# Per-tile order in a group norm's end, and a second PSUM bank with a split last step in a state space model's end

## The reference, cut to what matters

```python
mean = jnp.mean(y, axis=-1, keepdims=True)               # over a head of 64 channels
var = jnp.mean(jnp.square(y - mean), axis=-1, keepdims=True)
yn = ((y - mean) * lax.rsqrt(var + RW_GN_EPS)).reshape(B, T, D)
yn = yn * ln_w.astype(f32) + ln_b.astype(f32)
bonus = jnp.sum(rh * kh * r_k.astype(f32), axis=-1, keepdims=True) * vh
out = (yn + bonus.reshape(B, T, D)).astype(x.dtype) * g
return out @ w_o, v_first
```

```python
y = (einsum("blgp,ghp->blgh", s_re, c_re) - einsum("blgp,ghp->blgh", s_im, c_im) + d * uf)
y = jax.nn.gelu(y)
cu = jax.nn.silu(layer_norm(cu, conv_ln_g, conv_ln_b))
```

## Time and profile before

| | |
|---|---|
| median of 3 runs | 3901.69 us (3901.31 to 3909.06) |
| profiled execution | 3902.99 us, its span 3901.2 us |
| TensorE busy | 3577.1 us (92%) |
| VectorE busy | 2570.5 us (66%) |
| ScalarE busy | 1536.5 us (39%) |
| GpSimd busy | 1152.7 us (30%) |
| mean granted TensorE clock | 0.965 |
| group norm's end | from 2027.9 us to the first product of `at[2]` at 2110.91 us |
| the model's end | from 3567.1 us (`outputs(2)`) to the barrier behind 3602.4 us |

### The profile page before, as it was taken

One profiled execution on the slowest core, in us unless ns is written; L12 is line 12 of the kernel. 1 busy time (PEld: TensorE's weight loads), 2 busy tenths in 40 slices (PEclk: granted clock), 3 DMA queues, 4 the chain that ended last, 5 costly groups with the idle time before them and its releaser, 6 DMA issues. The chain is left out here.

```text
span 3901.2 us, 57647 instructions
## 1 busy us (share of the span) xinstructions
PE 3577.1 (92%) x24956; PEld 2905.9 (74%) x24956; DVE 2570.5 (66%) x2287; ACT 1536.5 (39%) x1634; POOL 1152.7 (30%) x521
## 2 busy tenths in 40 slices
PE   8999999999989998877777999999998999997997
PEld 6778788878767776666655788878886888875775
DVE  5554767687756857766655666678758888816532
ACT  5563432344534338744444433343443222113312
POOL 1125454555421211233322445445520000000211
PEclk9999999999999999999998999999999999997998
DMA  2112233344212245712113123253312222231322
GB/s 97 49 38 62 70 108 104 104 158 171 68 55 82 107 144 163 237 63 73 69 46 113 46 98 111 92 185 131 115 48 106 75 75 78 82 141 30 144 95 103
DMA packets 187037, 383.74 MB, mean 98 GB/s; under 512 B 16080, under 2 KB 84816, under 8 KB 181008
## 3 DMA queue, kind: packets, MB, share of 16 engines
q1 hardware_dynamic: 149216, 307.68, 23.8%
q10 hardware_dynamic: 37568, 72.36, 5.0%
HBM read 273.57 MB, written 105.91 MB: 97 GB/s over the span
## 5 line engine op out<-in xcount | busy, mean ns | idle before, releaser
L3817 POOL MEMSET ssm_toep<- 128x4096 f32 x1 | 3.5, 3512 | 545.7 <-POOLq L3516 545.7
L3403 DVE SCALAR_TENSOR_TENSOR H<-hy_cu,par,H 128x1024 f32<-128x1024 f32 x120 | 153.5, 1279 | 0.0
L269 POOL TENSOR_TENSOR wlo1C<-fast_raw,whi1C 128x1024 fp32r<-128x1024 f32 (+1 forms) x40 | 110.9, 2773 | 113.4 <-ACT whi1C L259 113.4
L269 POOL TENSOR_TENSOR wlo0B<-fast_raw,whi0B 128x1024 fp32r<-128x1024 f32 (+1 forms) x40 | 112.1, 2802 | 107.5 <-ACT whi0B L259 107.5
L3403 DVE SCALAR_TENSOR_TENSOR hy_odd<-hy_cu,par,hy_odd 128x1024 f32<-128x1024 f32 x112 | 143.3, 1280 | 0.0
L269 POOL TENSOR_TENSOR wlo1A<-fast_raw,whi1A 128x1024 fp32r<-128x1024 f32 (+1 forms) x40 | 111.4, 2785 | 105.6 <-ACT whi1A L259 105.6
L269 POOL TENSOR_TENSOR wlo1B<-fast_raw,whi1B 128x1024 fp32r<-128x1024 f32 (+1 forms) x39 | 107.9, 2766 | 114.3 <-ACT whi1B L259 114.3
L1007 DVE TENSOR_TENSOR fast_xl<-fast_xr,fast_xh 128x2048 fp32r<-128x2048 f32 (+1 forms) x42 | 127.5, 3059 | 21.3 <-ACT fast_xh L848 21.3
L269 POOL TENSOR_TENSOR wlo0A<-fast_raw,whi0A 128x1024 fp32r<-128x1024 f32 (+1 forms) x40 | 110.1, 2753 | 105.0 <-ACT whi0A L259 105.0
L269 POOL TENSOR_TENSOR wlo0C<-fast_raw,whi0C 128x1024 fp32r<-128x1024 f32 (+1 forms) x39 | 108.0, 2770 | 104.2 <-ACT whi0C L259 104.2
L942 DVE TENSOR_TENSOR fast_g<-fast_g,flow_rms 128x1024 f32<-128x1024 f32 x44 | 127.0, 2886 | 1.5
(11 more groups left out here) (1458 smaller groups left out, 11925.8 us busy)
## 6 DMA issues: line engine op xcount, KB each, us to landing
fast_raw<-ffn_in_dram SPq DMA_DIRECT2D x88, 512.0 KB, 3.8
fast_xr<-ffn_x SPq DMA_DIRECT2D x28, 1024.0 KB, 6.1
sc_ops<-rw_arbkv SPq DMA_DIRECT2D x15, 1280.0 KB, 7.2
fast_raw<-ffn_out_dram SPq DMA_DIRECT2D x32, 512.0 KB, 3.8
wraw1A<-hybrid_in_dram SPq DMA_DIRECT2D x24, 512.0 KB, 3.4
wraw1B<-hybrid_in_dram SPq DMA_DIRECT2D x24, 512.0 KB, 3.3
ffn_x<-fast_g ACTq DMA_DIRECT2D x22, 512.0 KB, 3.3
ffn_x<-fast_e ACTq DMA_DIRECT2D x22, 512.0 KB, 2.8
```

Of the source, the lines that this page charges most:

```text
L269: eng.tensor_tensor(self.slot(wlo, n), self.raw[n], self.slot(whi, n).bitcast(fp32), ALU.subtract)\
L3403: op = dve.scalar_tensor_tensor(out=acc, in0=c[:, j:j + T], scalar=w, in1=acc, op0=ALU.mult, op1=ALU.add)
L3817: pl.memset(toep[:, :, :], 0.0).then_inc(*tick("st_zero"))
```

## The change

In the group norm's end the three engines go tile by tile. VectorE does `gated(0)`, centres tiles 6 and 7, then `gated(k)` and `low(k - 1)` in turn. ScalarE takes `high(k)` between the roots. TensorE does `spreads(2)` ahead of all products and `spreads(3)` behind the product of tile 1. The low parts stay on VectorE.

In the state space model's end the outputs of odd k go to psC instead of psD, and wait for the copy of k - 2 rather than k - 1. The last `outputs(3)` is cut into two halves with `back(2)` between them. `back(3)` goes to psB and waits for the Ln that read psB. VectorE copies `outputs(2)` ahead of the scaled tiles, and makes six scaled tiles ahead of the copy of `outputs(3)` and two behind it.

```diff
                     sums(3)
-                    for q in range(DT // 2):
-                        if q == 0:
-                            W.begin(pe, at[0])
-                            W.begin(pe, at[1])
-                        for k in (2 * q, 2 * q + 1):
-                            pe.wait_ge(*after("ro_lo", k + 1))
-                            W.product(pe, at[0], k, *self.xs[k])
-                            W.product(pe, at[1], k, *self.xs[k])
-                        if q < 2:
-                            spreads(q + 2)
+                    spreads(2)
+                    W.begin(pe, at[0])
+                    W.begin(pe, at[1])
+                    for k in range(DT):
+                        pe.wait_ge(*after("ro_lo", k + 1))
+                        W.product(pe, at[0], k, *self.xs[k])
+                        W.product(pe, at[1], k, *self.xs[k])
+                        if k == 1:
+                            spreads(3)
...
                     squares(2)
+                    high(0)
                     roots(1)
-                    for q in range(DT // 2):
-                        high(2 * q)
-                        high(2 * q + 1)
-                        if q == 0:
-                            squares(3)
-                        if q + 2 < DT // 2:
-                            roots(q + 2)
+                    high(1)
+                    squares(3)
+                    high(2)
+                    roots(2)
+                    high(3)
+                    roots(3)
+                    high(4)
+                    high(5)
                     W.hi(act, 2)
+                    high(6)
+                    high(7)
...
-                    for q in range(DT // 2):
-                        gated(2 * q)
-                        gated(2 * q + 1)
-                        low(2 * q)
-                        low(2 * q + 1)
-                        if q == 0:
-                            centre(DT - 2)
-                            centre(DT - 1)
+                    gated(0)
+                    centre(DT - 2)
+                    centre(DT - 1)
+                    for k in range(1, DT):
+                        gated(k)
+                        low(k - 1)
+                    low(DT - 1)
...
-                        def outputs(k):
+                        def outputs(k, groups=range(8)):
...
+                            elif k == 1:
+                                pe.wait_ge(*after("sb_b", SU))
                             else:
-                                pe.wait_ge(*after("sy_c", 2 * k))
+                                pe.wait_ge(*after("sy_c", 2 * k - 2))
...
-                                to = ps[3][:, g % 2, q * P:(q + 1) * P]
+                                to = ps[3 - k % 2][:, g % 2, q * P:(q + 1) * P]
...
-                            pe.wait_ge(*after("su_c", SU) if k == 0 else after("sy_t", k))
+                            if k == 0:
+                                pe.wait_ge(*after("su_c", SU))
+                            elif k < SU - 1:
+                                pe.wait_ge(*after("sy_t", k))
+                            else:
+                                pe.wait_ge(*after("ln_log", 1))
...
-                        for k in range(SU + 1):
-                            if k < SU:
-                                outputs(k)
-                            if k > 0:
-                                back(k - 1)
-                            if k == 0:
-                                variance(0)
-                                variance(1)
-                            if k == 1:
-                                for m in range(2, DT):
-                                    variance(m)
+                        outputs(0)
+                        variance(0)
+                        variance(1)
+                        outputs(1)
+                        back(0)
+                        for m in range(2, DT):
+                            variance(m)
+                        outputs(2)
+                        back(1)
+                        outputs(3, range(4))
+                        back(2)
+                        outputs(3, range(4, 8))
+                        back(3)
...
-                        for k in range(4):
-                            normed(k)
                         outputs(2)
-                        for k in range(4, DT):
+                        for k in range(6):
                             normed(k)
                         outputs(3)
+                        for k in range(6, DT):
+                            normed(k)
```

More of the change, by code:

```diff
@@ L3855, in outputs @@
                                 pe.wait_ge(*after("st_in", 16 * SC))
-                            else:
-                                pe.wait_ge(*after("sy_c", 2 * k))
-                            for g in range(8):
+                            elif k == 1:
+                                pe.wait_ge(*after("sb_b", SU))
+                            else:
+                                pe.wait_ge(*after("sy_c", 2 * k - 2))
+                            for g in groups:
                                 q, rows = g // 2, slice(64 * (g % 2), 64 * (g % 2) + 64)
-                                to = ps[3][:, g % 2, q * P:(q + 1) * P]
+                                to = ps[3 - k % 2][:, g % 2, q * P:(q + 1) * P]
                                 pe.matmul(to, ut[:, 8 * k + g, :], toep[:, 8 * k + g, :], start=True, stop=False)
@@ L3863, in outputs @@
                                     mm = pe.matmul(to, ee[rows, k, z, q, 0:SN], cq[rows, k, z, q, SSM_H:], start=False, stop=(z == 1))
-                            mm.then_inc(*tick("pe_yc"))
+                            if groups[-1] == 7:
+                                mm.then_inc(*tick("pe_yc"))
                         def back(k):
                             pe.wait_ge(*after("sy_c", 2 * k + 2))
-                            pe.wait_ge(*after("su_c", SU) if k == 0 else after("sy_t", k))
+                            if k == 0:
[4 more added lines that the diff above has]
+                                pe.wait_ge(*after("ln_log", 1))
                             for i in range(SC):
-                                mm = pe.transpose(ps[0][:, i // 4, (i % 4) * P:(i % 4 + 1) * P],
+                                mm = pe.transpose(ps[k // (SU - 1)][:, i // 4, (i % 4) * P:(i % 4 + 1) * P],
                                                   yc[:, k, i, :, :].rearrange("p g h -> p (g h)"), ident)
@@ L3949, in _ @@
                             act.wait_ge(*after("pe_yt", k + 1))
-                            act.activation(y[:, k, :].rearrange("p (c i) -> p i c", i=SC), flat[0].rearrange("p (i c) -> p i c", i=SC),
+                            act.activation(y[:, k, :].rearrange("p (c i) -> p i c", i=SC), flat[k // (SU - 1)].rearrange("p (i c) -> p i c", i=SC),
                                            ACT.Gelu_apprx_tanh).then_inc(*tick("sy_t"))
@@ L3997, in outputs @@
                                 dve.tensor_copy(yc[:, k, :, e:8:2, :].rearrange("p i q h -> p q i h"),
-                                                ps[3][:, e, :].rearrange("p (q i h) -> p q i h", q=4, i=SC)).then_inc(*tick("sy_c"))
+                                                ps[3 - k % 2][:, e, :].rearrange("p (q i h) -> p q i h", q=4, i=SC)).then_inc(*tick("sy_c"))
                         ch(dve.memset(ee[:, :, :, :, 0:1], 0.0))
```

## The result

The change makes the kernel faster: 3873.01 us, the median of 4 runs (3864.44 to 3876.89), against 3901.5 (4 runs, 3899.82 to 3909.06) beside it, a ratio of 0.9922 with an interval of 0.9905 to 0.9938. Forecast were 3875 and a range of 3869 to 3884. The profiled execution took 3864.44 us, 38.5 less than the one of before (3902.99); it is the fastest of the four.

What follows compares the result with a forecast made beforehand. VectorE's order of work was taken to bound the group norm's end, and TensorE's wait for a copy and the lower clock the model's end. Gains of 15.2 + 11.6 = 26.8 us gave 3875 us, range 3869 to 3884.

Steps and rivals of the forecast that it cites:

- VectorE binds the first place: Group norm's end: VectorE's 41.6 us of work, two 0.8 us waits and 2.3 us of blocking set its end; gain 15.2 us.
- The collision: Group norm's end: GpSimd's low part of strip 2 blocks a VectorE operation through the shared port pair, costing 2.3 us.
- Rival (c): Group norm's end: GpSimd and VectorE do not collide; whole gain 29.1 us, time 3872.6; chance 0.08.
- The waits of TensorE: Group norm's end: TensorE's waits for the low parts shrink from 26.1 to some 15 us, each 1 to 4 us.
- The windows show a clock near 1.00: Group norm's end: the new profile's windows would show TensorE's granted clock near 1.00.
- no gap of 7 us is left: Group norm's end: TensorE's gaps become 1 to 3 us instead of 7 to 10, an argument against a low clock.
- rival (b): Group norm's end: clock falls between single products and stays low, TensorE binds; gain 5.2 there, 16.8 in all, 3884.9; chance 0.08.
- The model's end: State space model's end: `outputs(3)` follows `back(1)` without a wait and the clock stays at 1.00; gain 11.6 us.
- (a): Model's end: the clock falls though the gap is gone; gain 6.2 there, 21.4 in all, 3880.3; chance 0.13.
- The gain kept: Behind the group norm's end: TensorE has no gap for 44.1 us, so the 15.2 us gained there stay in the total.
- (d): Behind the group norm's end: its gain is given back later, only the model's end counts; 3890.1; chance 0.05.
- (e): Six strips of `at[2:]`: clock stays low there too, each strip losing 9.5 us; slower, 3942 with all six; chance 0.02.

Runs made afterwards that it cites:

- the filled gap: Changed group norm, old model's end, plus 12 unread products in TensorE's gap behind `back(1)`: first product of `outputs(2)` to SP's next-stage issue 27.42 us, 35.58 before.
- the bank alone: Changed group norm; of the model's end only psC/psD alternation, old orders kept: first product of `outputs(2)` to SP's next-stage issue 24.26 us, 24.18 with the whole change.
- The crossed kernels: Whole change with strip 2 late, but pairs kept with early centring, or tile order with late centring: first gated operation to first psC product 49.30 and 59.40 us.
- the four small edits: Against before: tiles 6 and 7 centred early, spreads(2) and spreads(3) one place earlier, pairs kept; psC for odd outputs: 3870.86 us, ratio 0.9915.

## Why the prediction was right, and where it wasn't

**VectorE binds the first place: right.** 41.6 us of work and two waits of 0.8 us were forecast; the waits are 0.88 and 0.81, at the root and at the high part that I named. psC's first product is 50.00 us behind the start, forecast 50.3 (2095.7 - 2045.42). The time itself came within 2 us of the 3875 forecast, and that is partly luck: the four executions lie between 3864.44 and 3876.89. The distances are the better test.

**The collision: right, a little smaller.** 2.3 us forecast; the operation took 2.0 us more than alone, and moving GpSimd away gave 1.99. Rival (c) is out. The Trainium skill's rule on the shared port pair ("SBUF — State Buffer", section "SBUF: two separate sides") agrees with it, and with the seven long operations of the kernel with low parts on GpSimd.

**The waits of TensorE: too large.** Some 15 us were forecast, 9.8 measured, in six waits. It was no term of the sum; TensorE's idle time ahead of the last low part changes nothing.

**"The windows show a clock near 1.00", "no gap of 7 us is left": the clock was wrong.** It fell to 0.61, 0.72 and 0.76 in windows behind gaps of only 2.37, 2.79 and 2.43 us. So the observation of rival (b) came true, and its price didn't: there the clock had to stay low for all eight tiles, so that TensorE bound. It came back within some us each time and was at 1.00 from 2083 on, when the last tiles came, and until then TensorE waited for VectorE at either clock. The Trainium skill, "TensorE: Matmul & The Clock Gate", section "A second HAM failure mode: psum-queue depth-cycling", says that short idles make the clock swing; the windows agree with that swing, though here the idles are waits for VectorE. What decides is who is late.

**The model's end: right, for the reason given.** 11.6 us forecast, 11.40 measured, and the clock stayed at 1.00 through `outputs(3)`, so (a) is out. The size of the clock's part, 8.2 of 11.4, is shown by the filled gap. One term was mis-sized: `back(3)` was put at 1.09 and took 1.97, at the lower clock. Half of it was made up elsewhere, which is luck: `outputs(3)` ended 18.5 us behind the start of `outputs(2)`, forecast 19.0 (3586.1 - 3567.1), as the products started 0.93 us behind the start of the transposes ahead of them and not 1.09. And much of what I costed step by step isn't needed: I put the split, the new order and psB into the chain, and the bank alone gives the same within 0.1 us. Measured from the first product of `outputs(2)`, VectorE's last copy starts after 18.57 us with the split, with `back(2)` inside, and without it `back(2)` starts after 17.63. From there to the end of the last gelu it is 5.35 us with the split (1.34 idle, 1.97, 2.0 and handovers) and 6.36 without (1.09, 2.18 of wait, 1.06, 2.0). The sums are 23.92 and 23.99. Had `back(3)` run in 1.09, the split would have been worth 1.0.

**The gain kept: right, as far as the runs tell.** (d) would have needed the time between the two places to grow. It was 1456.2 us before and 1451.4 after. In three kernels it was about 1460, by the clock in `outputs(0)`, and one of these is the group norm's end alone; but four others with the same group norm's end took 1451.3 to 1451.9, so the loss doesn't follow from the changed group norm alone. That it comes more often with it can't be excluded: none of the three executions with a d1 above 59 us had it. The times alone leave room for some us of loss (6.6 to 18.3 us for this part). (e) had no basis either: from 2083 the clock was 1.00.

**The order by tile, the change's main stroke in the group norm, isn't what gives most of the gain.** The prediction named the chain, roots that wait for squares that wait for late centrings, but put each engine's order through as a whole and didn't ask which edit carries it. The crossed kernels do: the early centring and sums alone give 16.2 us, more than the 15.49 of the change, and the order by tile adds 1.3 and takes 2.0 back by the collision.

## What to carry to other kernels

When an engine with work enough waits for one that has less to do, look for what this one waits for in turn, and move that; here two centrings and four head sums of squares, made early, did what a rewritten order of three engines did. When a wait of TensorE is priced, price the clock behind it too, which was 8.2 of 11.4 us here, but only where TensorE is the one that is late. Judge an edit of 1 to 15 us in a kernel of 3900 by distances between fixed instructions (d1 repeated within 0.05 us in five kernels with the same code there), not by its total, which scatters by 5 to 21 us within one kernel. Even a distance holds its value only where the clock does the same each time: with the old model's end d2 was 35.58 and 34.91.

## What was not expected of the hardware

- The clock fell in windows behind idle times of 2.4 to 2.8 us in the group norm's end (0.61, 0.72, 0.76), where the prediction looked only at gaps of 7 us and more.
- Behind some 19 us of products without a pause at 1.00 the clock fell within the 1.38 us of idle time ahead of `back(3)` or just as it began, in every kernel with the split (1.83 to 1.97 us for eight transposes). In the kernel with the bank only, in the one with the four small edits and in the one with the gap filled it stayed at 1.00 over 2.18 us of idle time (1.06 us for the transposes). What makes the difference I can't say: the split kernels have `back(2)` in the middle, the others have it between the outputs and the idle time. No run was made for it.
- At the lower clock the 49 fp32 products of `outputs(3)` ran for 14.85 us without a gap in before, and the clock did not come back; no more did it in the 15.0 us of `outputs(0)` in three kernels. The products of the group norm's end had it back in a few us.
- The same code, behind the same wait of 10.8 us, met either level of the clock from execution to execution, and that moved the distance from `outputs(0)` to `outputs(1)` by 8.75 us, more than most of the edits tried here.
